# Key turning and its copies, moved from the end of the odd head to its middle, in a two-block transformer kernel

## The reference

```python
def causal_block_attention(q, k, v):
    ...
        s = jnp.einsum('bhqd,bhkd->bhqk', q_blk, k).astype(jnp.float32) * scale
        ...
        s = jnp.where(key_pos[None, :] <= query_pos[:, None], s, NEG_INF)
        p = jax.nn.softmax(s, axis=-1).astype(v.dtype)
        return jnp.einsum('bhqk,bhkd->bhqd', p, v)
```

## Time and profile before

| what | us |
|---|---|
| median of 3 runs | 1831.97 (1831.77 to 1832.18) |
| the profiled execution's own time | 1831.05 |
| its span in the profile | 1829.2 |
| PE busy in it | 1752.6 (96%) |
| DVE busy | 1239.3 (68%) |
| ACT busy | 926.6 (51%) |
| POOL busy | 486.0 (27%) |

### The profile page before, as it was taken

The page is one execution under the profiler, slowest core; times in us unless marked ns, Lnnn a source line. Parts: engine busy times, 40 slices in busy tenths (PEclk is TensorE's granted clock), DMA queues, the critical chain, the costliest instruction groups (busy, mean ns, idle before and its releaser), DMA issues.

```text
span 1829.2 us, 27614 instructions
## 1 busy us (share of the span) xinstructions
PE 1752.6 (96%) x10382; PEld 1430.3 (78%) x10382; DVE 1239.3 (68%) x1895; ACT 926.6 (51%) x1692; POOL 486.0 (27%) x383
## 2 busy tenths in 40 slices
PE   9999999999999877799999999999999999999997
PEld 6778799999887655568999988868766777866675
DVE  8964588886436756657888854476675677567657
ACT  6624466654225655546656532233466733356763
POOL 0960266763000000004767610033000202200010
PEclk9999999999999988999999999999999999999998
DMA  6323223233332110002232333323111123211111
GB/s 215 103 73 92 92 82 116 93 116 108 96 102 89 58 35 24 12 33 83 93 116 94 114 107 95 101 84 109 59 58 58 47 81 101 96 58 58 47 58 58
DMA packets 56464, 151.74 MB, mean 83 GB/s; under 512 B 16768, under 2 KB 18720, under 8 KB 56336
## 3 DMA queue, kind: packets, MB, share of 16 engines
q1 hardware_dynamic: 52816, 147.45, 24.6%
q0 software_dynamic: 3520, 2.57, 0.6%
HBM read 142.84 MB, written 4.19 MB: 80 GB/s over the span
## 4 chain that ended last, share of the span: by engine, by line
PE 82%; DVE 9%; ACT 4%; POOL 3%; issue 2%; DMA 0%; SPq 0%; DVEq 0%; ACTq 0%; POOLq 0%
PE bank L2495 10%; PE bank L2497 10%; PE bank L2496 10%; PE bank L2708 7%; PE bank L2710 7%; PE bank L2709 7%; PE bank L3080 3%; PE bank L3082 3%; PE bank L3081 3%; PE bank L3033 2%; PE bank L3062 2%; PE bank L3063 2%; PE bank L3064 2%; PE bank L2788 1%; DVE wl L1572 1%
## 5 line engine op out<-in xcount | busy, mean ns | idle before, releaser
L1572 DVE TENSOR_TENSOR wl<-raw,wh 128x1024 fp32r<-128x1024 f32 (+2 forms) x183 | 230.2, 1258 | 262.5 <-ACT wh L862 258.4
L862 ACT ACTIVATE wh<-raw 128x1024 fp32r<-128x1024 f32 (+2 forms) x183 | 188.6, 1030 | 354.6 <-PE bank L2497 288.2
L2495 PE MATMUL bank<-hidH,wh 128*128 128x512 f32 x352 | 137.4, 390 | 0.0
L2496 PE MATMUL bank<-hidL,wh 128*128 128x512 f32 x352 | 137.0, 389 | 0.0
L2497 PE MATMUL bank<-hidH,wl 128*128 128x512 f32 x352 | 136.9, 389 | 0.0
L2708 PE MATMUL bank<-xH,wh 128*128 128x256 f32 x480 | 135.8, 283 | 0.0
L2709 PE MATMUL bank<-xL,wh 128*128 128x256 f32 x480 | 135.8, 283 | 0.0
L2710 PE MATMUL bank<-xH,wl 128*128 128x256 f32 x480 | 135.8, 283 | 0.0
L773 POOL TENSOR_TENSOR raw<-raw,wsum 128x512 f32<-128x512 f32 x40 | 86.5, 2164 | 115.2 <-DVE wl L1901 115.2
L3080 PE MATMUL bank<-xH,wh 128*128 128x512 f32 x256 | 111.2, 435 | 6.0 <-ACT qk L1435 3.1
L3082 PE MATMUL bank<-xH,wl 128*128 128x512 f32 x256 | 100.8, 394 | 0.0
(11 more groups left out here) (525 smaller groups left out, 5133.1 us busy)
## 6 DMA issues: line engine op xcount, KB each, us to landing
raw<-w_gu_dram SPq DMA_DIRECT2D x88, 512.0 KB, 3.8
raw<-w_p_dram SPq DMA_DIRECT2D x64, 512.0 KB, 3.3
raw<-w_dn_dram SPq DMA_DIRECT2D x32, 448.0 KB, 3.4
raw<-w_glu_dram SPq DMA_DIRECT2D x16, 512.0 KB, 3.5
raw<-w_dn_dram SPq DMA_DIRECT2D x16, 512.0 KB, 3.6
raw<-w_out_dram SPq DMA_DIRECT2D x16, 512.0 KB, 3.2
raw<-w_in_dram SPq DMA_DIRECT2D x8, 512.0 KB, 7.6
raw<-w_o_dram SPq DMA_DIRECT2D x8, 512.0 KB, 3.2
```

The costliest lines, as they stand in the source:

```text
L862: nc.scalar.activation(wh[:, (st.base + u) % 2, 0:kts * P], raw[:, (st.base + u) % 4, 0:kts * P], ACT.Copy).then_inc(w_high, 1)
L1572: nc.vector.tensor_tensor(wl[:, s, 0:kts * P], raw[:, (st.base + u) % 4, 0:kts * P], wh[:, s, 0:kts * P].bitcast(F32), ALU.subtract).then_ ...
L2495: nc.tensor.matmul(bank, wh[:, s, w], hi[:, k, :], start=first and kt == 0, stop=False)
L2496: nc.tensor.matmul(bank, wh[:, s, w], lo[:, k, :], start=False, stop=False)
```

## The change

The order of two calls changes, one on PE and one on ScalarE, in odd heads 1, 3, 5, 7, 9 and 11.

```diff
@@ -1316,13 +1316,13 @@
                     if h + 1 < NH:
                         probs(h + 1, 1 - s, j)
+                    if j == 2 and s and pair + 2 < NH // 2:
+                        take_keys(pair + 2)
                     if 1 <= j <= len(units):
                         root_of_unit(units[j - 1])
                         ahead_of_unit(units[j - 1])
                     if j < len(units):
                         unit_square(units[j])
-                if s and pair + 2 < NH // 2:
-                    take_keys(pair + 2)
@@ -2961,6 +2961,8 @@
                     turn_probs(h, j)
                     if h + 1 < NH:
                         scores(h + 1, j)
+                    if j == 1 and s and pair + 2 < NH // 2:
+                        turn_keys(pair + 2)
                     if j < len(units):
                         unit(units[j])
...
-                if s and pair + 2 < NH // 2:
-                    turn_keys(pair + 2)
```

## The result

| kernel | median, us | runs |
|---|---|---|
| before | 1831.87 | 4 (1831.04 to 1832.18) |
| changed | 1848.74 | 4 (1846.02 to 1850.4) |

The ratio is 1.0091, with a 95% interval of 1.0074 to 1.0109: the change costs 16.9 us where 8.1 were forecast, and the time lies above the range. The profiled execution took 1848.2 us, its span 1846.3.

A forecast was written before the change was run, and what follows sets the result against it. PE's own work was taken to bound the kernel (82% of the chain). Heads 1, 3, 5, 7, 9, 11 lose 2.0 + 2.3 + 2.0 + 0.7 + 0.8 + 0.3 = 8.1 us, clock zero: 1840.0 us, range 1834.0 to 1844.0.

The forecast's parts named there:

- 5.05 and 8.75 us: Stepwise lengths from L2100's end to the next head's first probabilities: 5.05 in heads 7 and 11, 8.75 in 3 and 5.
- The clock. ... I count zero: PE's clock behind odd heads: splitting the pause into two shorter ones may save or add falls, 1.5 us each; counted zero.
- The bound of +3.0: Upper bound of the clock term: two more falls of PE's clock added, +3.0 us.
- The ceiling on the gain: End waits for the key copies: a mean of 1.67 us in six odd heads, about 10 us at most.
- A: Rival, 12%: clock kept in heads 7, 11 and perhaps 5, as no pause is long enough; +3.6 to +5.1 us.
- B: Rival, 7%: queries taken early enough that PE loses nothing in mid-head; -10 to -4.4 us, between 1822 and 1828.
- C: Rival, 8%: VectorE's slack takes up most of the hold in heads with units, two clock falls saved; -3 to +3.6 us.
- D: Rival, counted nothing: the change does not do what it says; end wait stays, hold comes on top, above the range.

The follow-up runs named there:

- e1: The change with only PE's key turning moved, ScalarE's copies left at the odd head's end: 1854.59 us, against 1833.71 for the kernel before.
- e2: Only ScalarE's copies moved, behind the exponential of block 2, PE's list as in the kernel before: 1830.32 us against its 1833.71.
- e3: The change with VectorE taking the queries between row minima 0 and 1 in odd heads: 1827.20 us, against 1833.71 for the kernel before.
- e11: The change with both unread matmuls in the hold and the last unit scaled before the sharing in heads 6 and 10: 1840.17 us, kernel before 1833.17.
- e4: The change with three unread 128x512 matmuls ahead of the key turning, filling PE's hold: 1843.44 us, against 1833.71 for the kernel before.
- e12: The kernel before with three unread matmuls ahead of the query turning of heads 2 to 12 (even): 1821.65 us against its 1833.17.
- e9_scale_first: The change with VectorE scaling the last unit ahead of the sharing in heads 6 and 10: 1847.96 us, against 1831.98 for the kernel before.
- e5: The kernel before with only ScalarE's copies moved, straight ahead of the exponential of block 3, keys turned at the end: 1827.61 us against its 1831.98.
- e13: The change with queries taken early, copies ahead of block 3's exponential, early scaling in heads 6 and 10, and unread matmuls in remaining waits: 1815.43 us, kernel before 1831.87.

## Why the prediction was wrong in size and right in kind

*What bounds it, and where the loss comes from: right.* Slower was forecast, by a new wait of PE's key turning for L2100, "2 to 3 us in each of six heads, some 15 in all"; the trace has 15.4 in six. That this hold is the loss, and not the copies, is shown by e1 (worse than the change), e2 (a gain) and e3 (the loss gone with the hold). The lengths from L2100's end to the next head, 5.05 and 8.75 us, hold in head 11 (4.95) and, with the clock held, in heads 3 and 7. e11 has the sum: 7.0 measured (4 to 9), 8.1 forecast.

*The step that failed: "The clock. ... I count zero".* The term was 6 to 7 us by e4. I had set the falls that a shorter pause at the end would save against those that a pause in the middle would add, as if they were of one kind. They aren't: in heads 3 and 7 the clock fell behind the hold, when PE had two turnings and two scores queued, in head 3 a unit too, with VectorE and ScalarE waiting for them, so that most of the slowed work was on the path (the unit of head 3 alone 1.27 us; the filled hold gives back 1.5 us in head 3 and 1.0 in head 7). And the pauses at the end of heads 1 and 5 did not get shorter but longer, from 4.42 and 4.46 to 5.00 and 5.37 us, with a low clock as before. The bound of +3.0 was two added falls; the clock fell behind four of the six holds.

The rule of the Trainium skill, "TensorE: Matmul & The Clock Gate", "Why this matters for your kernels", that long idle gaps cause the drops, is borne out only in part. The low clock comes behind pauses of PE here, and goes when they are filled (e4, e12). But the length of the pause alone does not tell whether the clock falls: in the changed kernel it fell behind those of 2.08 us (head 1), 2.94 (3) and 2.68 (5 and 7), and stayed full behind 2.68 (9) and 2.35 (11), while in e9_scale_first it stayed full behind head 7's 2.68 and was low behind head 11's 2.35. The row of head 7, in the timeline of the changed kernel, ahead of the window shown above:

```profile
748.83 0.63 PE L2880 MATMUL bank<-cons,k_rows 128*128 128x128 f32 x4 [2.68 <-issue]
```

What I drew from it, that splitting a pause keeps the clock, was wrong in heads 1, 3, 5 and 7. Heads 9 and 11 kept it behind the hold in this execution, which by e9 is partly luck.

*The step that was missing:* in heads 5 and 9 the working ended at VectorE's sharing. The query turning ahead in PE's queue waits for L2091, which VectorE runs behind the sharing. The view of waits before has that wait ("PE bank L2870 <- DVE q_rows L2091: 7.8, 2, 4.5", above), and I had taken heads 5 and 9 like 3 and 7. The ceiling on the gain had the same fault: it counted six heads, and in e5 heads 5 and 9 gain nothing from earlier copies. It was worth 1.7 and 1.4 us by e4, of which the early scaling gives back 1.0 each. What the rest is, 0.7 and 0.4, wasn't tried.

*The rivals.* A (the clock kept) did not come; B (the hold covered) came true only where I made it so, in e3, where L2100 is over before PE comes to the keys: 6.5 us below the kernel before, B's -4 to -10. C and D did not come.

## What to carry to other kernels

Before an operation is moved ahead in an in-order queue, list its waits at the new place, and everything queued behind it that others wait for: a buffer that is free at the end of a loop may be full in its middle. The consumer of that buffer can often be moved with it at little cost, and then the move pays. Price a new pause of PE at its length and at the slowed matmuls behind it, most of all if these are what the other engines wait for. Check for each head or iteration apart which of several waits ends last, not only in the one that was worked through.

## What was not expected of the hardware

Adding work made the kernel faster: three unread 128x512 matmuls in each of six waits took 11.5 us off the kernel before, without a change to any other engine's list. With the granted clock at 1.00 instead of 0.83, head 8, an even head with one unit, took 8.72 us instead of 10.29. Over the whole span the mean clock only went from 0.989 to 0.996, so a mean that looks nearly full can hide falls that cost 0.6% of the time. And a fill pays only where the wait that guards its bank is already met: the one in head 0 of e13 started the head 3.7 us late.
